# Stick-breaking weights from sigmoids and a backward scan on VectorE, in a two-layer trunk

## The reference

```python
z = einsum('bhqd,bhsd->bhqs', q_blk, k) * scale
mask = key_pos[None, :] < t[:, None]              # strictly causal
sp = where(mask, softplus(z), 0.0)
log_w = log_sigmoid(z) - (cumsum(sp, axis=3, reverse=True) - sp)
w = where(mask, exp(log_w), 0.0)
o = einsum('bhqs,bhsd->bhqd', w, v)
```

## Time and profile before

| | |
|---|---|
| median of 3 runs | 1094.82 us (1094.5 to 1095.06) |
| the profiled execution's own time | 1095.11 us |
| its span in the profile | 1093.3 us |
| mean granted TensorE clock | 1.00 |
| TensorE busy | 99% |
| VectorE busy | 63% |
| ScalarE busy | 46% |
| GpSimd busy | 6% |

### The profile page before, as it was taken

How to read it: one execution, slowest core, us unless ns; L and a number is a source line. 1 busy time by engine, 2 the same in 40 slices (tenths; PEclk the granted TensorE clock), 3 DMA queues, 4 the chain that set the end, 5 groups by cost and what they waited for, 6 DMA issues and landing times.

```text
span 1093.3 us, 15107 instructions
## 1 busy us (share of the span) xinstructions
PE 1083.1 (99%) x5998; PEld 918.3 (84%) x5998; DVE 691.2 (63%) x920; ACT 501.8 (46%) x714; POOL 69.9 (6%) x62
## 2 busy tenths in 40 slices
PE   9999999999999999999999999999999999999997
PEld 7886889998888888888899877998888888888886
DVE  7675777788776767622257777398876767661313
ACT  6556966555343444322235466454444444441321
POOL 3000001230000000001103000121000000000000
PEclk9999999999999999999999999999999999999999
DMA  6323232213222222223322623212222222221322
GB/s 230 116 78 77 78 116 78 78 43 112 82 111 86 106 89 103 83 91 106 107 81 82 166 94 116 83 73 78 85 108 89 104 92 100 97 96 58 116 97 77
DMA packets 22919, 105.49 MB, mean 96 GB/s; under 512 B 4048, under 2 KB 6480, under 8 KB 12240
## 3 DMA queue, kind: packets, MB, share of 16 engines
q1 hardware_dynamic: 22720, 104.71, 28.1%
q10 hardware_dynamic: 144, 0.01, 0.0%
HBM read 98.02 MB, written 2.10 MB: 92 GB/s over the span
## 4 chain that ended last, share of the span: by engine, by line
PE 92%; DVE 4%; ACT 2%; DMA 1%; issue 1%; SPq 1%; DVEq 0%
PE ps L1673 29%; PE ps L1675 28%; PE ps L1674 28%; PE ps L1856 1%; PE ps L1869 1%; PE ps L1892 1%; DVE ps L1443 1%; PE ps L2162 1%; DVE x L1449 1%; PE ps L2173 1%; DVE hx_lo L1453 1%; DVE w_lo L1169 1%; PE ps L2189 1%; ACT w_hi_s L725 1%; ACT prob L1075 0%
## 5 line engine op out<-in xcount | busy, mean ns | idle before, releaser
L1673 PE MATMUL ps<-hx_hi,w_hi 128*128 128x512 f32 x812 | 320.0, 394 | 1.0 <-DVE w_lo L1169 0.9
L1675 PE MATMUL ps<-hx_hi,w_lo 128*128 128x512 f32 x812 | 316.4, 390 | 0.0
L1674 PE MATMUL ps<-hx_lo,w_hi 128*128 128x512 f32 x812 | 316.3, 390 | 0.0
L1122 DVE TENSOR_TENSOR w_lo<-w_raw,w_hi 128x2048 fp32r<-128x2048 f32 (+1 forms) x74 | 167.7, 2266 | 122.1 <-ACT w_hi L725 121.9
L725 ACT ACTIVATE w_hi<-w_raw 128x2048 fp32r<-128x2048 f32 (+1 forms) x76 | 142.0, 1870 | 109.0 <-DMA w_raw<-in_ffn_w_down 90.7
L1673 PEld LDWEIGHTS ps<-hx_hi,w_hi 128*128 128x128 f32 x812 | 152.4, 188 | 38.0 <-issue 6.5
L1675 PEld LDWEIGHTS ps<-hx_hi,w_lo 128*128 128x128 f32 x812 | 152.4, 188 | 31.9
L1674 PEld LDWEIGHTS ps<-hx_lo,w_hi 128*128 128x128 f32 x812 | 152.5, 188 | 31.0 <-issue 0.5
L984 ACT ACTIVATE cg<-ug,vec 128x512 f32<-128x512 f32 x44 | 35.9, 816 | 140.7 <-DVE ug L1489 140.7
L996 ACT ACTIVATE g_hi<-cv 128x512 f32 (+1 forms) x44 | 27.8, 632 | 111.1 <-DVE cv L1507 111.1
L1498 DVE SCALAR_TENSOR_TENSOR cg<-ug,vec,cg 128x511 f32<-128x511 f32 x88 | 65.8, 748 | 20.4 <-ACT cg L984 20.4
(11 more groups left out here) (284 smaller groups left out, 1948.9 us busy)
## 6 DMA issues: line engine op xcount, KB each, us to landing
w_raw<-in_ffn_w_up SPq DMA_DIRECT2D x40, 1024.0 KB, 4.8
w_raw<-in_ffn_w_down SPq DMA_DIRECT2D x16, 1024.0 KB, 4.8
w_raw<-in_even_w_in SPq DMA_DIRECT2D x6, 1024.0 KB, 4.9
w_raw<-in_even_w_out SPq DMA_DIRECT2D x3, 1024.0 KB, 4.8
w_raw_s<-in_odd_w_qkv SPq DMA_DIRECT2D x3, 1024.0 KB, 4.8
w_raw<-in_odd_w_qkv SPq DMA_DIRECT2D x3, 1024.0 KB, 5.4
w_raw<-in_odd_w_o SPq DMA_DIRECT2D x3, 1024.0 KB, 5.4
rsw<-rp SPq DMA_DIRECT2D x40, 64.0 KB, 2.0
```

The source lines that it names most:

```text
L1122: dve.tensor_tensor(w_lo[s][:, 0:k], w_raw[s][:, 0:k], w_hi[s][:, 0:k], ALU.subtract).then_inc(w_lo_done, 1)
L1673: pe.matmul(dst, s_hi, r_hi, start=first, stop=False)
L1674: pe.matmul(dst, s_hi, r_lo, start=False, stop=False)
L1675: return pe.matmul(dst, s_lo, r_hi, start=False, stop=last)
```

## The change

**Attention.** Queries now lie on the partitions and keys on the columns: `sb_z` makes for each query block q one matmul over all its 128 (q + 1) keys, eight for a pair, and no mask. ScalarE takes two sigmoids out of PSUM, taken = sigmoid(z) and keep = sigmoid(-z) (`sb_sigmoids`). VectorE's `sb_weights` runs a scan from the last key to the first, in four pieces, one per query block: state = max(state x keep of the key to the right, nearest), where nearest is a loaded constant with a one at the key just before the query; it writes over the scores in PSUM. A product of 1280 columns with taken gives the weights. TensorE turns them, ten transposes of 128x128 a head (`sb_turn`), into PSUM, ScalarE copies them to SBUF (`sb_copy`), and `sb_av` makes four matmuls a head instead of five. Softplus, the splits, the tails, `sb_cum` and the constants for them are gone.

`sb_turn(2p)` stands in half 7 + 4p, after its k tile 4, 4, 9 or 6 (pair 2's half is of a v unit, with 16 such places), `sb_turn(2p + 1)` in half 8 + 4p after k tile 2. For pair 3, `sb_turn(7)` comes after `out_whole`, and `sb_av(3)` between the two `out_half` stretches of unit 11.

**Recurrent branch.** The square of lru_a goes from VectorE to ScalarE (after the decays). The tables that ScalarE loads ahead are those of the sigmoid instead of those of the logarithm.

**Start.** The pieces become ten: k tiles 0, 1, 2 and 3, 4 and 5, 6 and 7 of each of two units. The first two go through ScalarE's queue instead of SyncE's, and VectorE instead of ScalarE casts piece 0. VectorE (`first_sum`) instead of GpSimd adds the first squares. `keep_warm` makes four matmuls, eight passes, instead of five.

The diff, cut to its core.

Places, pieces and loads, and ScalarE at the start:

```diff
-    tri_r, ones_r, ident_r, mask_r = (const_r[:, P * i:P * i + P] for i in range(4))
+    nearest = place("nearest", [P, T], F32)
...
-    TAIL = 3 * P
-
-    def block_at(j, q):
-
-        return {0: 0, 1: T, 2: 2 * T}[q - j] + P * j if q - j < 3 else T + TAIL
+    ROWS_AT = {3: 0, 2: T, 0: 2 * T - P, 1: 2 * T}
+    KEYS_AT = {j: ROWS_AT[TT - 1 - j] for j in range(TT)}
...
+    sig = [inbig(f"sig{e}", [P, 2 * SPAN], F32) for e in range(2)]
+    keep, taken = ([t[:, SPAN * i:SPAN * i + SPAN] for t in sig] for i in range(2))
+    w_keys = keep
...
+    FIRST_K = [(0, 1), (1, 2), (2, 4), (4, 6), (6, 8)]
+    LAST_PIECE = 2 * len(FIRST_K) - 2
+
     def first_piece(n):
-
-        return n % 2, slice(2 * (n // 2), 2 * (n // 2) + 2)
+        return n % 2, slice(*FIRST_K[n // 2])
...
+    def load_piece(engine, n):
+        u, ks = first_piece(n)
+        engine.dma_start(w_raw[u][:, ks].rearrange("p k b n -> p k (b n)"), io["even_w_in"][4 + 2 * u][:, ks]).then_inc(first_in[n], 16)
...
-        for q in range(4):
-            load_x(2 * q)
-            if q:
-                load_x(2 * q + 1)
-            load_piece(2 * q)
-            load_piece(2 * q + 1)
-            if q == 0:
-                load_x(1)
+        load_x(0)
+        load_x(1)
+        load_piece(sp_, 2)
+        load_piece(sp_, 3)
+        for q in (2, 4, 6):
+            load_x(q)
+            load_piece(sp_, 2 + q)
+            load_piece(sp_, 3 + q)
+            load_x(q + 1)
...
-        pre_norm(0)
         whole_sums(0, 2)
...
+        load_piece(act, 0)
+        load_piece(act, 1)
         act.preload_act_table_set("sqrt_and_others")
         act.wait_ge(pregain_in, 16)
         first_hx_hi(0)
-        first_split_hi(0)
+        act.wait_ge(first_hi, 1)
         first_split_hi(1)
         first_hx_hi(1)
+        first_split_hi(2)
+        first_split_hi(3)
```

ScalarE in the attention stage:

```diff
-        def sb_softplus(h):
+        def sb_sigmoids(h):
 
             act.wait_ge(z_mm, h // 2 + 1)
             if h >= 2:
-                act.wait_ge(cum_mm, h - 1)
-            t = sp[h % 2]
-            act.activation(t[:], z_of(h), ACT.Abs).then_inc(abs_done, 1)
-            act.wait_ge(abs_done, h + 1)
-            act.activation(t[:], t[:], ACT.Exp, scale=-1.0).then_inc(exp_done, 1)
-            act.wait_ge(exp_done, h + 1)
-            act.activation(t[:], t[:], ACT.Ln, bias=1.0).then_inc(ln_done, 1)
-
-        def sb_hi(h):
-            act.wait_ge(sp_done, h + 1)
-            if h >= 2:
+                act.wait_ge(w_turned, h - 1)
                 act.wait_ge(av_mm, h // 2)
-            act.activation(sp_hi[h % 2][:], sp[h % 2][:], ACT.Copy).then_inc(sp_hi_done, 1)
-
-        def sb_tail_hi(h):
-            act.wait_ge(tail_done, h + 1)
-            act.activation(tail_hi[h][:], tail[h][:], ACT.Copy).then_inc(tail_hi_done, 1)
-
-        def sb_weights(h):
-            act.wait_ge(cum_mm, h + 1)
-            act.activation(z_s[h % 2][:], z_of(h), ACT.Exp).then_inc(w_done, 1)
+            act.activation(taken[h % 2], z_of(h), ACT.Sigmoid)
+            act.activation(keep[h % 2], z_of(h), ACT.Sigmoid, scale=-1.0).then_inc(sig_done, 1)
+
+        def sb_copy(h):
+
+            act.wait_ge(w_turned, h + 1)
+            act.activation(w_keys[h % 2], z_of(h), ACT.Copy).then_inc(w_copied, 1)
...
+            act.wait_ge(lru_dve, 1)
+            act.activation(xc[:], lru_a[:], ACT.Square).then_inc(lru_sq, 1)
...
         for p in range(PAIRS):
             for e in range(2):
-                sb_softplus(2 * p + e)
-            for e in range(2):
-                sb_hi(2 * p + e)
-                sb_tail_hi(2 * p + e)
+                sb_sigmoids(2 * p + e)
...
             for e in range(2):
-                sb_weights(2 * p + e)
+                sb_copy(2 * p + e)
```

VectorE at the start:

```diff
+        def first_sum(i):
+
+            dve.wait_ge(sq_done, i + 1)
+            if i == 1:
+                ins = dve.tensor_tensor(sumsq[:], sq[0][:], sq[1][:], ALU.add)
+            else:
+                dve.wait_ge(sum_done, i - 1)
+                ins = dve.tensor_tensor(sumsq[:], sumsq[:], sq[i % 2][:], ALU.add)
+            ins.then_inc(sum_done, 1)
+
+        dve.wait_ge(first_in[0], 16)
+        dve.tensor_copy(w_hi[0][:, 0:1], w_raw[0][:, 0:1]).then_inc(first_hi, 1)
         dve.wait_ge(pregain_in, 16)
         first_hx_lo(0)
         first_split_lo(0)
         first_split_lo(1)
         first_hx_lo(1)
+        first_split_lo(2)
+        first_split_lo(3)
         for i in range(2, DT):
             if i % 2 == 0:
-                first_split_lo(i)
+                first_split_lo(2 + i)
             first_hx_lo(i)
             if i % 2 == 0:
-                first_split_lo(i + 1)
-        dve.wait_ge(const_in, 32)
-        dve.tensor_scalar(tri_r[:], tri, -1.0, None, ALU.mult)
-        dve.tensor_scalar(ones_r[:], ones, -1.0, None, ALU.mult)
-        dve.tensor_copy(ident_r[:], ident)
-        dve.tensor_copy(mask_r[:], mask).then_inc(consts_cast, 1)
+                first_split_lo(3 + i)
+            if i >= 3:
+                first_sum(i - 2)
+        for i in (DT - 2, DT - 1):
+            first_sum(i)
```

VectorE in the attention stage:

```diff
+        def left_of(h, q):
+
+            a = T * sb_set(h) + ROWS_AT[q]
+            return ps[:, a:a + P * (q + 1)]
+
+        def sb_weights(h):
+
+            dve.wait_ge(sig_done, h + 1)
+            if h == 0:
+                dve.wait_ge(nearest_in, 16)
+            for q in (3, 2, 0, 1):
+                n, a = P * (q + 1), ROWS_AT[q]
+                ins = dve.tensor_tensor_scan(out=left_of(h, q)[:, ::-1], data0=sig[h % 2][:, a + 1:a + 1 + n][:, ::-1],
+                                             data1=nearest[:, T - n:T][:, ::-1], initial=0.0, op0=ALU.mult, op1=ALU.max)
+            ins.then_inc(left_done, 1)
+            dve.wait_ge(left_done, h + 1)
+            dve.tensor_tensor(taken[h % 2], bank(sb_set(h), 3)[:, 0:SPAN], taken[h % 2], ALU.mult).then_inc(w_done, 1)
...
-            sb_softplus(2 * p)
-            sb_tail(2 * p)
+            sb_weights(2 * p)
             evac(6 + 4 * p)
-            sb_softplus(2 * p + 1)
-            sb_lo(2 * p)
-            sb_tail_lo(2 * p)
-            sb_tail(2 * p + 1)
-            sb_lo(2 * p + 1)
-            sb_tail_lo(2 * p + 1)
+            sb_weights(2 * p + 1)
             evac(7 + 4 * p)
...
-                dve.tensor_tensor(xc[:], lru_a[:], lru_a[:], ALU.mult).then_inc(lru_dve, 1)
-                dve.wait_ge(lru_dve, 2)
+                dve.wait_ge(lru_sq, 1)
```

TensorE:

```diff
-        keep_warm(5)
+        keep_warm(4)
...
-            if k % 2 == 0:
-                piece_wait(pe, k, first_lo, w_lo_done)
-                piece_wait(pe, k + 1, first_lo, w_lo_done)
+            n = {1: 2, 2: 4, 4: 6, 6: 8}.get(k)
+            if n is not None:
+                piece_wait(pe, n, first_lo, w_lo_done)
+                piece_wait(pe, n + 1, first_lo, w_lo_done)
...
-            for j, q in [(j, j + n) for n in range(TT) for j in range(TT - n)]:
+            for q in (3, 2, 0, 1):
                 for e in range(2):
                     rows = slice(HD * e, HD * e + HD)
-                    c0 = T * sb_set(e) + block_at(j, q)
-                    pe.matmul(ps[:, c0:c0 + P], kT[p][rows, P * j:P * j + P], qT[rows, p, P * q:P * q + P],
-                              start=j == 0 and q < 3, stop=False, skip_group_check=True)
-            for e in range(2):
-                last = pe.matmul(bank(sb_set(e)).rearrange("p (j c) -> p j c", c=P), ident_r[:],
-                                 mask_r[:].unsqueeze(1).broadcast_to([P, TT, P]), start=False, stop=False, skip_group_check=True)
+                    c0 = T * sb_set(e) + ROWS_AT[q]
+                    last = pe.matmul(ps[:, c0:c0 + P * (q + 1)], qT[rows, p, P * q:P * q + P], kT[p][rows, 0:P * (q + 1)],
+                                     start=q > 0, stop=q < 2, skip_group_check=True)
             last.then_inc(z_mm, 1)
...
+        def sb_turn(h):
+
+            pe.wait_ge(w_done, h + 1)
+            c0 = T * sb_set(h)
+            for j in range(TT):
+                for q in range(j, TT):
+                    c = c0 + KEYS_AT[j] + P * (q - j)
+                    last = pe.transpose(ps[:, c:c + P], taken[h % 2][:, ROWS_AT[q] + P * j:ROWS_AT[q] + P * j + P], ident)
+            last.then_inc(w_turned, 1)
+
+        def turn_at(h, at):
+
+            return lambda k: sb_turn(h) if k == at else None
 
         def sb_av(p):
 
-            pe.wait_ge(w_done, 2 * p + 2)
+            pe.wait_ge(w_copied, 2 * p + 2)
             if p in (0, 2):
                 pe.wait_ge(half_evac, 6 if p == 0 else 16)
-            for j, q0, q1 in ((0, 0, 3), (0, 3, 4), (1, 1, 4), (2, 2, 4), (3, 3, 4)):
+            for j in range(TT):
                 for e in range(2):
                     c = HD * (2 * p + e)
-                    last = pe.matmul(bank(SB_OUT)[HD * e:HD * e + HD, P * q0:P * q1], v0[:, j, c:c + HD], weights_of(e, j, q0, q1),
-                                     start=j == q0 == 0, stop=j == TT - 1, skip_group_check=True)
```

(74 more changed lines are left out.)

61 lines of the change are left out of this document (10 added, 51 removed).

## The result

The changed kernel takes 1099.45 us, median of 5 runs (1098.19 to 1100.46), against 1095.06 (1094.50 to 1095.28): ratio 1.004, 95% interval 1.0028 to 1.0053. Beside later experiments it took 1099.17 (1098.20 to 1102.57), ratio 1.0038 (1.0024 to 1.0052). So the changed kernel is 0.4% slower, 4.4 us, where the forecast was 1.6 us less; 1099.45 is above the range, on the side that had 0.19. Its profiled execution took 1098.19 us, span 1096.4, mean granted clock 0.995 against 1.00. One run of experiment 4 took 3829.35 us and is left out of its median.

A forecast was written before the change was run, and what follows sets the result against it. TensorE was taken to bound the kernel, busy 1083.1 of 1093.3 us. Terms -9.1 - 0.4 - 1.6 + 0.8 + 2.2 + 5.7 + 0.8 = -1.6 us gave a median of 1093.2; 8-in-10 range 1089.5 to 1097.0.

The forecast's parts named there:

- the side that had 0.19: The whole kernel measurably slower than before: chance 0.19, against 0.37 for faster and 0.44 for no telling difference.
- rivals A to D: VectorE's weights 3.0 a head, 1088.6 (0.18); 6.0, 1099.6 (0.10); scores not overlapping, 1101 (0.05); 275 ns transposes, 1106 (0.02).
- D: Attention's 80 transposes on TensorE take 275 ns each: +13 us, 1106; chance 0.02.
- The slow restart: TensorE may run slow after idling before unit 11: 0.8 us, bounds 0 and 1.6, from ten warm passes at the start.
- rival E: Behind unit 11's wait: no slow restart gives 1092.4, all of it 1094.0; both lie in the forecast, no separate chance.
- a wait of "0.8" before the gates: TensorE waits at the gates for the swapped copy of xc: 0.8 us, bounds 0 and 1.5.
- The landing of the copy: Swapped xc's two transfers, behind a load on SyncE, land 8.8 and 10.2 us after issue.
- The cover of the start: At the start, keep_warm loses 2 of 10 passes, which end before the first matmul either way; no cost.
- the wait on VectorE: At the start, TensorE's wait at 23.37 us for VectorE's split goes with the sums on VectorE: 0.85 us gained.

The follow-up runs named there:

- experiment 4: The changed kernel's attention with the start of the kernel before (pieces, queues, casts, sums, warm passes): 1098.26 us, ratio 1.003.
- Experiment 3: The changed kernel plus 40 unread products on TensorE between the last transposes and unit 11: 1096.23 us, ratio 1.0007.
- experiment 2: The changed kernel with the two transfers of the swapped xc issued ahead of the load of unit 8: 1094.91 us, ratio 0.9997.
- experiment 5: The changed kernel as it is, run again beside later variants on one chip: 1099.17 us, runs 4.4 us apart.
- experiments 9 and 10: The 1084.86 us kernel of all four moves, first with keep_warm(6), 12 passes: 1085.41 us; then with the start of the kernel before: 1086.40 us.

## Why the prediction was wrong

Its accounting of work held. Mask and sums are gone, a turn takes 1.01 us (1.09 forecast), TensorE waits at none of the turns, and the scores take 2.36 us (2.43 before). VectorE's weights take 4.4 us a head (4.55): scans 2.97 and a product 1.49. So none of the rivals A to D happened. D's 275 ns, which the Trainium skill states for a 128x128 bf16 transpose in one kernel's context ("TensorE: Matmul & The Clock Gate", Part 4), is 101 ns for the fp32 ones here. The waits before `out_whole` (1.52 against 2.2) and before unit 11 (5.45 against 5.7) were found and sized from before. Three steps failed.

**The slow restart was mis-sized.** The prediction took "half, 0.8" of 1.6 us, once, behind unit 11's wait. It was 1.6 behind the gates and 2.2 behind unit 11, 3.8 in all, beyond its upper bound of 1.6, and rival E (the clock alone, 1092.4 to 1094.0) was too narrow with it. Experiment 3 takes the second away while the wait stays; experiment 2 takes the first with its wait. The row that gave the bound counted the whole loss of ten warm passes, which end when real work starts; it could not show how long the state goes on behind a wait. And a wait of "0.8" before the gates was given no restart at all. The Trainium skill ("TensorE: Matmul & The Clock Gate", Part 1) says that an idle array returns to 1.2 GHz, and here the granted clock of 0.50 agrees; the wait of 1.52 us did not bring it down, those of 2.75 and 5.45 did. Over all profiles a wait of 2.11 brought it down and one of 2.69 did not (experiment 5), so no fixed price could have been right in every run.

**The landing of the copy was taken as fixed.** That "they land 8.8 and 10.2 us after issue" was one observation of two transfers behind a load. After the change they took 9.4 and 11.4, then 10.0 and 11.9 in the second profile, and the wait 2.75 and 3.2 instead of 0.8, past the bound of 1.5. Over the seven profiles that have them behind the load, the second landed after 10.8 to 11.9. Why these are slower than before by up to 1.7 us is not settled. Experiment 2 shows that with another place in the queue, ahead of the load and 11 us earlier, they land in 4.4 and 6.3; it does not part the load from the moment.

**The cover of the start was costed at nothing.** The prediction said that the warm passes "end before the first matmul either way". They do, and the gap behind them is part of the cost, beside the landing itself. The piece's landing, not hx_hi, sets the first matmul (5.12 to 6.07 instead of 4.7), and by the first scores the start is worth -1.1 or +0.6 to +1.2 us instead of -1.6. With the gap filled it is worth 1086.40 - 1085.41 = 1.0 us (experiments 9 and 10). Part of the -1.6, the wait on VectorE, can count only in the early kind of start.

Together, for the first profile: 2.0 more at the gates, 3.8 - 0.8 = 3.0 more clock, 0.5 less gain at the start, 0.9 less wait in the tail, 0.55 less in the rest: some 4.0 of the 4.7 us between -1.6 and +3.1. Pairs 0 and 2 saved 2.23 each where the steps gave 2.38; four such pairs make another 0.6. The median of the runs is another 1.3 higher: the first profile was of the fastest run, and the start and the gates go by luck.

## What to carry to other kernels

When work in front of a wait is cut, follow every follower to its queue: here a copy behind a load and a cast behind a copy each cost more than the 2.2 us saved in a pair, and with them and two more moved, +4.4 us became -10.3 (1084.86 against 1095.15 beside it). Price a wait on TensorE with what the clock does behind it, as a range: 2.75 us of waiting cost 4.3, 5.45 cost 7.7, but 2.69 once cost no more than itself, and 3.19 cost 5.9. And to make the runs even, fill the time before the first data lands until its latest landing, not its usual one.

## What was not expected of the hardware

With eight warm passes, the first matmuls ran at half rate until some 10 us in the five profiles with a gap of 0.55 to 1.07 us behind the passes; in the two with 0.21 and 0.45 they were at full rate from 6.1 us or earlier, and so they were from the start with 12 and 14 passes, which left no gap. The granted clock reads 1.00 in these stretches all the same, so at the start only the durations show it.

A backward scan into PSUM takes 2.97 us for 1280 columns in four pieces, 2.3 ns a column, about the rate of the forward scans in SBUF (2.2).
